# Delta rule inverse on 32 by 32 tiles instead of 64 by 64

## What is computed

```python
m = jnp.where(strict, jnp.einsum('nbhid,nbhjd->nbhij', kb, kc) * decay, 0.0)
a = m + jnp.eye(C)
u_c = lax.linalg.triangular_solve(a, vb, left_side=True, lower=True, unit_diagonal=True)
```

## Time and profile before

| | us |
|---|---|
| median of 3 runs (lowest, highest) | 3049.61 (3045.38, 3055.71) |
| the profiled execution, its time | 3034.23 |
| its span, first to last instruction | 3032.9 |
| TensorE busy in the span | 2904.1 (96%) |
| mean granted clock of TensorE | 0.971 |

### The profile page before, as it was taken

How to read it: one execution, slowest core, us unless ns; L and a number is a source line. 1 busy time by engine, 2 the same in 40 slices (tenths; PEclk the granted TensorE clock), 3 DMA queues, 4 the chain that set the end, 5 groups by cost and what they waited for, 6 DMA issues and landing times.

```text
span 3032.9 us, 55258 instructions
## 1 busy us (share of the span) xinstructions
PE 2904.1 (96%) x23638; PEld 2767.9 (91%) x23638; DVE 2009.5 (66%) x2887; ACT 1229.0 (41%) x1633; POOL 337.2 (11%) x331
## 2 busy tenths in 40 slices
PE   7999999899999997998999999999999999999999
PEld 4888888899999887998999989899999999998998
DVE  4686775777776697677655865676565476647654
ACT  2222222445444243434544422445454454134643
POOL 5000001201002121003101020011020101000301
PEclk9999999899999998999999999999999999999999
DMA  7353443689996785898656623356576654233654
GB/s 271 108 178 117 143 148 110 186 246 283 256 257 205 209 247 178 250 275 239 181 165 170 163 61 95 105 150 181 166 196 171 178 154 112 85 101 109 181 164 129
DMA packets 747377, 524.77 MB, mean 173 GB/s; under 512 B 19370, under 2 KB 711788, under 8 KB 747004
## 3 DMA queue, kind: packets, MB, share of 16 engines
q1 hardware_dynamic: 743004, 516.18, 59.1%
q0 software_dynamic: 4128, 5.06, 0.6%
HBM read 520.07 MB, written 2.94 MB: 172 GB/s over the span
## 4 chain that ended last, share of the span: by engine, by line
PE 78%; DVE 9%; ACT 6%; issue 5%; DMA 1%; SPq 0%; POOL 0%; DVEq 0%; ACTq 0%; POOLq 0%
PE bank L496 21%; PE bank L497 21%; PE bank L498 21%; ACT weights_hi L466 4%; PE bank L618 2%; DVE conv_out L2281 1%; DVE weights_lo L476 1%; PE bank L843 1%; PE bank L1439 1%; PE bank L755 1%; PE bank L2456 1%; PE bank L2448 1%; PE bank L1523 1%; PE bank L2460 1%; PE bank L1154 1%
## 5 line engine op out<-in xcount | busy, mean ns | idle before, releaser
L476 DVE TENSOR_TENSOR weights_lo<-weights_raw,weights_hi 128x2048 fp32r<-128x2048 f32 (+3 forms) x414 | 854.6, 2064 | 365.4 <-ACT weights_hi L466 364.6
L466 ACT ACTIVATE weights_hi<-weights_raw 128x2048 fp32r<-128x2048 f32 (+3 forms) x414 | 709.6, 1714 | 644.9 <-PE bank L498 519.8
L496 PE MATMUL bank<-ffn_in_hi,weights_hi 128*128 128x256 f32 x1184 | 342.5, 289 | 14.0 <-DVE ffn_in_lo L1217 9.0
L498 PE MATMUL bank<-ffn_in_hi,weights_lo 128*128 128x256 f32 x1184 | 338.7, 286 | 0.0
L497 PE MATMUL bank<-ffn_in_lo,weights_hi 128*128 128x256 f32 x1184 | 338.4, 286 | 0.0
L496 PE MATMUL bank<-mac_in_hi,weights_hi 128*128 128x256 f32 x1024 | 289.3, 283 | 1.6 <-DVE mac_prod L2064 1.2
L497 PE MATMUL bank<-mac_in_lo,weights_hi 128*128 128x256 f32 x1024 | 289.6, 283 | 0.0
L498 PE MATMUL bank<-mac_in_hi,weights_lo 128*128 128x256 f32 x1024 | 288.9, 282 | 0.0
L496 PE MATMUL bank<-mix_in_hi,weights_hi 128*128 128x256 f32 x960 | 280.9, 293 | 6.2 <-DVE mix_in_lo L1965 3.7
L497 PE MATMUL bank<-mix_in_lo,weights_hi 128*128 128x256 f32 x960 | 273.8, 285 | 0.0
L498 PE MATMUL bank<-mix_in_hi,weights_lo 128*128 128x256 f32 x960 | 273.7, 285 | 0.0
(11 more groups left out here) (442 smaller groups left out, 7215.5 us busy)
## 6 DMA issues: line engine op xcount, KB each, us to landing
weights_raw<-in_ffn_w SPq DMA_DIRECT2D x132, 512.0 KB, 6.2
weights_raw<-in_w_in SPq DMA_DIRECT2D x120, 512.0 KB, 5.1
side_weights<-in_ada_w SPq DMA_DIRECT2D x86, 576.0 KB, 4.4
weights_raw<-in_ffn_wg SPq DMA_DIRECT2D x88, 512.0 KB, 4.0
weights_raw<-in_ffn_wu SPq DMA_DIRECT2D x88, 512.0 KB, 5.3
weights_raw<-in_ffn_wd SPq DMA_DIRECT2D x64, 704.0 KB, 4.7
weights_raw<-in_ffn_w SPq DMA_DIRECT2D x48, 704.0 KB, 7.0
side_weights<-in_ada_w SPq DMA_DIRECT2D x112, 256.0 KB, 3.1
```

Of the source, the lines that this page charges most:

```text
L466: k.s.activation(k.w_hi[s % HIGHS][:, 0:n], k.raw[s % RING][:, 0:n], ACT.Copy).then_inc(*k.hi.up())
L476: k.v.tensor_tensor(k.w_lo[s % RING][:, 0:n], k.raw[s % RING][:, 0:n], k.w_hi[s % HIGHS][:, 0:n].bitcast(F32), ALU.subtract).then_inc(*k.l ...
L496: k.te.matmul(out, l[0], r[0], start=first, stop=False)
L498: return k.te.matmul(out, l[1], r[0], start=False, stop=last)
```

## The change

The levels run on tiles of 32 by 32: four for each head and half, at partitions 0, 32, 64 and 96, again on the diagonal of the array. There are four levels (pairs to 32). X and its transpose of a half lie side by side in one buffer (256 columns each), and their two updates in one PSUM bank, so that one subtraction of 512 columns serves both. The step from 32 to 64 is made like the corner: the product of M's off-diagonal block with X (tiles 0 to 1 and 2 to 3), a copy by ACT (y32), a fill, the products with the transposes, and negations from PSUM into their places. X's top tile of 64 is put together by ACT (two small copies for a half) and DVE, with POOL's cleared part. The corner from 64 to 128 stays. The mask table gets 6 tables of 32 columns for 6 of 64, plus one identity of 32. Of the diff, cut:

```diff
-NLEV = 7
+QUARTER = P // 4
+NLEV = 5
...
 def pe_inverse(k):
...
         for i in range(DN_H):
-            for r in ROWS:
-                m = te.matmul(AB[2 * tt][r, BLK[i]], XTc[r, tt, i, :], k.ident[r, r], start=True, stop=True)
+            for q in Q:
+                m = te.matmul(AB[2 * tt][q, QBLK[i]], XT32[tt][q, i, :], k.ident[q, q], start=True, stop=True)
         m.then_inc(*k.inv_turned.up())
-    for j in range(1, NLEV - 1):
+    for j in range(1, NLEV):
...
             for i in range(DN_H):
-                for r in ROWS:
-                    m = te.matmul(AB[2 * tt][r, BLK[i]], MT[r, i, tt * T + r.start:tt * T + r.stop], Xc[r, tt, i, :],
+                for q in Q:
+                    m = te.matmul(AB[2 * tt][q, QBLK[i]], MT[q, i, tt * T + q.start:tt * T + q.stop], X32[tt][q, i, :],
                                   start=True, stop=True)
             m.then_inc(*k.inv_times.up())
         pe_fill(k)
         for tt in range(2):
             te.wait_ge(*k.inv_masked.at(2 * (j - 1) + tt + 1))
             for i in range(DN_H):
-                for r in ROWS:
-                    m = te.matmul(AB[2 * tt + 1][r, BLK[i]], XTc[r, tt, i, :], Y[tt][r, i, :], start=True, stop=True)
-            m.then_inc(*k.inv_right.up())
+                for q in Q:
+                    te.matmul(AB[2 * tt + 1][q, QBLK[i]], XT32[tt][q, i, :], Y32[tt][q, i, :], start=True, stop=True)
             for i in range(DN_H):
-                for r in ROWS:
-                    m = te.matmul(AB[2 * tt][r, BLK[i]], Y[tt][r, i, :], XTc[r, tt, i, :], start=True, stop=True)
-            m.then_inc(*k.inv_left.up())
+                for q in Q:
+                    m = te.matmul(AB[2 * tt + 1][q, QLEFT[i]], Y32[tt][q, i, :], XT32[tt][q, i, :], start=True, stop=True)
+            m.then_inc(*k.inv_stepped.up())
         pe_fill(k)
+    for tt in range(2):
+        te.wait_ge(*k.inv_joined.at(2 * (NLEV - 2) + tt + 1))
+        for i in range(DN_H):
+            for a, b in ((0, 1), (2, 3)):
+                m = te.matmul(AB[2 * tt][Q[b], QBLK[i]], MT[Q[a], i, tt * T + Q[b].start:tt * T + Q[b].stop],
+                              X32[tt][Q[a], i, :], start=True, stop=True)
+        m.then_inc(*k.inv_times.up())
+    pe_fill(k)
+    for tt in range(2):
+        te.wait_ge(*k.corner_kept.at(tt + 1))
+        for i in range(DN_H):
+            for a, b in ((0, 1), (2, 3)):
+                te.matmul(AB[2 * tt + 1][Q[a], QBLK[i]], Y32[tt][Q[b], i, :], XT32[tt][Q[b], i, :], start=True, stop=True)
+            m = te.matmul(AB[2 * tt + 1][Q[1], QBLK[i]], XT32[tt][Q[1], i, :], Y32[tt][Q[1], i, :], start=True, stop=True)
+        m.then_inc(*k.inv_stepped.up())
+    pe_fill(k)
+    te.wait_ge(*k.xt_cleared.at(4))
+    for tt in range(2):
+        te.wait_ge(*k.tiles_spread.at(tt + 1))
+        te.wait_ge(*k.inv_joined.at(2 * (NLEV - 1) + tt + 1))
...
 def act_inverse(k):
...
+    for _ in range(1, NLEV):
         act_hi(k)
     for tt in range(2):
+        s.wait_ge(*k.inv_times.at(2 * (NLEV - 1) + tt + 1))
+        s.activation(k.y32[tt], tiles(k.AB[2 * tt]), ACT.Copy).then_inc(*k.corner_kept.up())
+    for tt in range(2):
+        s.wait_ge(*k.inv_joined.at(2 * (NLEV - 2) + tt + 1))
+        s.activation(k.xc[Q[0], tt, :, 0:QUARTER], k.x32[tt][Q[0], :, :], ACT.Copy)
+        s.activation(k.xc[Q[1], tt, :, QUARTER:HALF], k.x32[tt][Q[1], :, :], ACT.Copy).then_inc(*k.tiles_spread.up())
+    act_hi(k)
+    for tt in range(2):
         s.wait_ge(*k.inv_corner.at(tt + 1))
...
 def pool_inverse(k):
...
+    for part in (k.xc[Q[0], :, :, QUARTER:HALF], XT[Q[1], :, :, Q[0]], XT[Q[3], :, :, Q[2]], XT[LOW, :, :, TOP]):
+        g.wait_ge(*k.xt_cleared.now())
+        g.memset(part, 0.0).then_inc(*k.xt_cleared.up())
...
 def dve_inverse(k):
...
     for tt in range(2):
+        for q in Q:
+            v.tensor_tensor(k.xt32[tt][q, :, :], MT[q, :, tt * T + q.start:tt * T + q.stop],
+                            k.lev[0][q, :].unsqueeze(1).broadcast_to([QUARTER, DN_H, QUARTER]), ALU.mult).then_inc(*k.dve.up())
+        v.wait_ge(*k.dve.now())
+        v.tensor_tensor(k.xt32[tt], bc(k.small_ident, DN_H), k.xt32[tt], ALU.subtract).then_inc(*k.inv_begun.up())
     dve_fill(k)
-    for j in range(1, NLEV - 1):
+    for j in range(1, NLEV):
         for tt in range(2):
             v.wait_ge(*k.inv_times.at(2 * (j - 1) + tt + 1))
+            v.tensor_tensor(k.y32[tt], tiles(k.AB[2 * tt]), bc(k.lev[j], DN_H), ALU.mult).then_inc(*k.inv_masked.up())
         dve_fill(k)
         for tt in range(2):
-            x, xt = flat(k.xc[:, tt]), flat(XTc[:, tt])
-            v.wait_ge(*k.inv_right.at(2 * (j - 1) + tt + 1))
-            v.tensor_tensor(x, x, k.AB[2 * tt + 1][:, :], ALU.subtract)
-            v.wait_ge(*k.inv_left.at(2 * (j - 1) + tt + 1))
-            v.tensor_tensor(xt, xt, k.AB[2 * tt][:, :], ALU.subtract).then_inc(*k.inv_joined.up())
+            both = flat(k.xtc[:, tt])
+            v.wait_ge(*k.inv_stepped.at(2 * (j - 1) + tt + 1))
+            v.tensor_tensor(both, both, k.AB[2 * tt + 1][:, :], ALU.subtract).then_inc(*k.inv_joined.up())
     v.wait_ge(*k.inv_joined.now())
     for tt in range(2):
-        for r in ROWS:
-            v.tensor_copy(XT[r, tt, :, r], XTc[r, tt])
+        for q in Q:
+            v.tensor_copy(XT[q, tt, :, q], k.xt32[tt][q, :, :])
+    dve_fill(k)
+    for tt in range(2):
+        v.wait_ge(*k.inv_stepped.at(2 * (NLEV - 1) + tt + 1))
+        for out, q in ((k.xc[Q[1], tt, :, 0:QUARTER], Q[1]), (XT[Q[2], tt, :, Q[3]], Q[2]), (XT[Q[0], tt, :, Q[1]], Q[0])):
+            m = v.tensor_scalar(out, tiles(k.AB[2 * tt + 1], q), -1.0, None, ALU.mult)
+        m.then_inc(*k.inv_joined.up())
...
+    k.x32, k.xt32, k.y32 = ([quarters(x) for x in xs] for xs in (
+        (k.xtc[:, 0, 0:4, :], k.xtc[:, 1, 0:4, :]), (k.xtc[:, 0, 4:8, :], k.xtc[:, 1, 4:8, :]),
+        (k.y2[0][:, 0:4, :], k.y2[1][:, 0:4, :])))
```

More of the change, by code:

```diff
@@ L90, in shape_tables @@
     strict = np.concatenate([(p[:, None] < t[None, :]), (p[:, None] < p[None, :])], 1).astype(float)
-    lev = []
-    for j in range(NLEV - 1):
-        row, col = (p % HALF)[:, None] >> j, np.arange(HALF)[None, :] >> j
+    lev = [(p % QUARTER)[:, None] == np.arange(QUARTER)[None, :]]
+    for j in range(NLEV):
+        row, col = (p % QUARTER)[:, None] >> j, np.arange(QUARTER)[None, :] >> j
         low = (row // 2 == col // 2) & (row % 2 == 1) & (col % 2 == 0)
@@ L274, in __init__ @@
         self.corner_kept = self.sig("corner_kept", "act")
+        self.tiles_spread = self.sig("tiles_spread", "act")
+        self.inv_stepped = self.sig("inv_stepped", "pe")
         self.decay_exp = self.sig("decay_exp", "act")
@@ L2422, in dve_scores, with quarters, tiles @@
                                    ALU.mult, ALU.mult).then_inc(*k.score_taken.up())
-ROWS = [slice(0, HALF), slice(HALF, P)]
+TOP, LOW = slice(0, HALF), slice(HALF, P)
+Q = [slice(i * QUARTER, (i + 1) * QUARTER) for i in range(4)]
 BLK = [slice(i * HALF, (i + 1) * HALF) for i in range(DN_H)]
+QBLK = [slice(i * QUARTER, (i + 1) * QUARTER) for i in range(DN_H)]
+QLEFT = [slice(T + i * QUARTER, T + (i + 1) * QUARTER) for i in range(DN_H)]
+def quarters(x):
+    return x.rearrange("p a (c n) -> p (a c) n", n=QUARTER)
+def tiles(bank, q=slice(0, P)):
+    return bank[q, 0:T].rearrange("p (a n) -> p a n", a=DN_H)
 def pe_inverse(k):
-    te, AB, MT, XTc, Xc, Y = k.te, k.AB, k.mt, k.xtc, k.xc, k.y2
+    te, AB, MT, XT32, X32, Y32 = k.te, k.AB, k.mt, k.xt32, k.x32, k.y32
     te.wait_ge(*k.before("dve"))
@@ L2471, in pe_inverse @@
     for tt in range(2):
-        te.wait_ge(*k.corner_kept.at(tt + 1))
+        te.wait_ge(*k.corner_kept.at(tt + 3))
         for i in range(DN_H):
-            m = te.matmul(AB[2 * tt + 1][top, BLK[i]], Y[tt][low, i, :], XTc[low, tt, i, :], start=True, stop=True)
+            m = te.matmul(AB[2 * tt + 1][TOP, BLK[i]], k.y2[tt][LOW, i, :], k.xt[LOW, tt, i, HALF:P], start=True, stop=True)
         m.then_inc(*k.inv_cornered.up())
 def act_inverse(k):
-    s, low = k.s, ROWS[1]
+    s = k.s
     for tt in range(2):
         s.wait_ge(*k.inv_turned.at(tt + 1))
-        s.activation(flat(k.xc[:, tt]), k.AB[2 * tt][:, :], ACT.Copy).then_inc(*k.inv_copied.up())
-    for _ in range(1, NLEV - 1):
+        s.activation(k.x32[tt], tiles(k.AB[2 * tt]), ACT.Copy).then_inc(*k.inv_copied.up())
+    for _ in range(1, NLEV):
         act_hi(k)
     for tt in range(2):
+        s.wait_ge(*k.inv_times.at(2 * (NLEV - 1) + tt + 1))
[6 more added lines that the diff above has]
+    for tt in range(2):
         s.wait_ge(*k.inv_corner.at(tt + 1))
-        s.activation(flat(k.y2[tt][:, :, :])[low, :], k.AB[2 * tt][low, :], ACT.Copy).then_inc(*k.corner_kept.up())
+        s.activation(flat(k.y2[tt][:, :, :])[LOW, :], k.AB[2 * tt][LOW, :], ACT.Copy).then_inc(*k.corner_kept.up())
 def pool_inverse(k):
-    k.g.wait_ge(*k.before("dve"))
-    k.g.wait_ge(*k.before("pe"))
-    k.g.memset(k.xt[ROWS[1], :, :, 0:HALF], 0.0).then_inc(*k.xt_cleared.up())
```

(17 more changed lines are left out.)

12 lines of the change are left out of this document (2 added, 10 removed).

## The result

The changed kernel takes 3075.68 us (median of 4 runs, 3069.15 to 3084.11), the kernel before beside it 3048.27: a ratio of 1.0088, 95% interval 1.0054 to 1.0122. It is slower by 27.4 us, where 21 us less were forecast.

What follows compares the result with a forecast made beforehand. TensorE was taken to bound two inverse stages of 74.47 us; gains of 2.4 + 8.3 + 0.5 = 11.2 us per layer, kept as 10.5, 21 in all, gave 3013 by the profiled execution, 3029 by the median; range 3020 to 3086.

Steps and rivals of the forecast that it cites:

- The price of a record: TensorE's small products on four 32x32 tiles: 7.9 ns per record by the column law, bounds 7.9 and 28.7.
- rival E: TensorE's small records: a fixed floor each, whatever their columns, 23.4 ns; 20 us slower in all, 3069; chance 0.16.
- The level's chain: Levels: ACT and DVE work through one subtraction sets the period, 9.9 us instead of 11.97; gain 8.3 us per layer.
- The start: Stage's begin: halves ready at 1.9 and 3.9 us, level 1's middle fill near 6.3 instead of 8.7; gain 2.4.
- The end: Last fill before the corner, with three negations from PSUM: 9.3 to 9.4 us instead of 9.96; gain 0.5.
- At nothing: Side work priced at zero: POOL's clears, ACT's and DVE's copies, a wait, the mask table, 1600 further TensorE instructions per layer.
- Rival B: TensorE's feed decides: records no faster than 28.7 ns, hurting from 18; 39 us slower, 3073 or 3088; chance 0.14.
- C: TensorE's array: only two tiles run at once, 15.8 ns per record; 3041 to 3045 us; chance 0.22 with its neighbours.
- D: Whole change: it does not do what it says, work only moved to the next stage; no size, given no chance.
- records over 18 ns apart: Sign in the stage's small records, named for Rival B and rival E; spacing above 18 ns.
- no idle in the levels: Sign in the levels, named for Rival B and rival E; the forecast itself had TensorE idle about 0.8 us there.
- stage over 75 us: Sign in the inverse stage's length, named for Rival B and rival E; the forecast itself said 63 to 65 us.

Runs made afterwards that it cites:

- the kernel with two kinds: Kernel before the change, with two of the three products of levels 1 to 4 on 32x32 tiles, the third on 64x64: stages 76.2 and 76.6 us.

## Why the prediction was wrong

The direction failed; 3075.68 lies in the range, which reached to 3086 for the rivals.

**The price of a record** was right: 8.7 ns against 7.9, with the bounds 7.9 and 28.7. The tile products fell by 11.6 us per stage instead of 15.3; 1.3 of the difference is that price (1664 x 0.8 ns), a part of the rest went to stretches at the lower clock. The Trainium skill (TensorE: Matmul & The Clock Gate, section "Wait — 56ns, not 53.3ns?") states a floor of about 25 ns from start to start, which rival E took over all tiles together; for records that alternate over four tiles it doesn't hold, they start 8.7 ns apart.

**The level's chain** was right where it could act: 9.98 us without the starved records. **The start** was nearly right but for the gap in it: DVE's four products of 256 elements took 1.76 us and the subtraction 0.43, so the second half was ready 4.4 us after the stage's begin, where 3.9 was said, and level 1's middle fill began at 8.8 us, 6.4 without the gap of 2.35, where 6.3 was said. **The end**: TensorE waited 2.4 us for the negations where 1.2 was in the sum, because the products of the step from 32 to 64 took 1.1 us and not the 2.0 they were given; the time of the end, 9.4 us from the fill to the corner, is the one forecast.

**The step that failed** stands under "At nothing": "The 1600 further TensorE instructions per layer need 102 kB more of instruction fetches [...]; no idle time of the stage is put down to them now". They cost 17.6 us of gaps per stage, and some 5.6 more in the fills through the lower clock behind the gaps. The lower clock behind the wait for the negations adds 2.3; that the clock would hold at 1.00 was taken for granted too. With the products' -11.6 and 1.4 more of waits for DVE the stage is +15.3, where the sum said -11.2. The argument took the absence of a wait in the old profile as a sign of room. Before, the densest stretch used a block in 3.7 us and the feed needs 3.5 to 3.8: the resource was at its limit in the bursts and showed nothing, because a level as a whole left it 11.97 us for 1.9 blocks.

**Rival B** was the one that came: "the feed of TensorE decides". Its mechanism as priced was off, an even 28.7 ns per record and fills that cost their own time beside it, 39 us for both layers and 3088 us. In truth the records run at 8.7 ns and stop, and the fills' few instructions do count, as relief: 24 dense matmuls are 48 instructions in 3 us. Its threshold of 18 ns per record was of no use for the same reason. Counted over a level, 864 instructions at its own figure of 14.4 ns are 12.4 us, and with 2.2 for the slab 14.6, against 14.8 measured; that 14.4 lies within the feed's 13.6 to 14.7 ns per instruction is luck, since it came from the columns of 64x64 tiles. B deserved more than 0.14. Rivals C and E are out by the 8.7 ns, D by the record counts.

The signs named were partly too weak: "records over 18 ns apart" never came, "no idle in the levels" was the opposite of what came, but "stage over 75 us" and the fall of the clock did.

## What to carry to other kernels

Count instructions as well as time when a product is cut into smaller ones: here half the tile side meant twice the records, one every 8.7 ns instead of 28.7, a rate of instructions 3.3 times as high. Take any stretch of 256 of TensorE's instructions and ask whether it lasts the 3.5 us that a block took here, or the 4.4 to 6.2 beside a large transfer. And a resource that the old profile never waits for may still be at its limit there; its rate in the densest stretch has to be compared with a measured one, here by a stream of small products at the end of the kernel.

## What was not expected of the hardware

- The fetch looks one block ahead at most: TensorE resumed 1.2 to 1.5 us behind the end of the fetch's own transfer (0.9 to 1.4 us long), and that began 0.4 to 1.4 us after TensorE had entered the block before, with a slab of 1 MB in transfer 1.9 to 3.6 us (first stage of the changed kernel, blocks of whose fetch TensorE had to wait for). The longest gap, at 1856.59, has such a fetch: block entered at 1855.50, transfer from 1859.07 to 1860.15, TensorE on at 1861.67. Free of slabs a block took 3.0 to 3.8 us, with one 4.4 to 6.2.
- Four tiles of 32x32 side by side bear a record every 8.7 ns, a weight load and a matmul, 4.4 ns an instruction, as long as the block lasts.
- In the changed kernel all nine gaps of 1.76 to 5.08 us were followed by a granted clock of 0.50, the 1.2 GHz level, and by fills of 0.21 us a matmul for 0.12; the gaps cost about a third of their own length again (5.6 of 17.6 us). In the second stage of the kernel with two kinds, gaps of 1.98 and 1.80 us left the clock at 1.00.
